# Eleven projections computed feature-major, and layer norms from chunk statistics

## The chip, the cores and the metric

The kernel runs on one core of a Trainium2 chip, in one launch. The metric is the device time of that launch in microseconds. All engine times below come from one profiled execution.

## The reference

Two blocks run one after the other on the same tokens (T = 256, model width 2048), in fp32. The first norms its input, projects it, and feeds a gated delta rule (8 heads of 128, causal convolution of 4 taps over q, k and v) and a block attention; both meet in a gated mix, an output projection and a feed-forward layer of width 5632. The second block has a differential attention layer and a forgetting attention layer, each followed by a layer norm. Cut to what the change touches:

```python
def _causal_short_conv(u, w):          # u: (1, T, 3072) = q, k, v projections of the delta rule
    y = up[:, 0:T] * w[0]              # up: u with three zero tokens in front
    for j in range(1, K):              # K = 4
        y = y + up[:, j:j + T] * w[j]
    return jax.nn.silu(y)
...
def layer_norm(x, g, b):
    mu = jnp.mean(xf, axis=-1, keepdims=True)
    var = jnp.mean(jnp.square(xf - mu), axis=-1, keepdims=True)
    y = (xf - mu) * lax.rsqrt(var + EPS)
    return (y * g + b).astype(x.dtype)
...
    sc = jnp.einsum('bqhcd,bkhcd->bhcqk', qb, k) + bias      # layer 0 of the second block (k2, q2)
    sc = jnp.einsum('bqhd,bkhd->bhqk', qb, k) + decay        # layer 1 (k3, q3)
...
    x = layer_norm(DN_ALPHA * x + gate[:, None] * y, ln_g[l], ln_b[l])
```

## The kernel before, in words

Every weight product runs in bodies of units. A unit is 256 rows by 512 columns of weights, 512 KB. SyncE loads it into one of four ring slots of `raw`; ScalarE rounds it to `w_hi` (`split`, L1105 to L1112), VectorE makes `w_lo = raw - w_hi` (L1704 to L1708), and TensorE multiplies both with the high and low parts of the operand, three fp32r matmuls per pair of tiles (`chunk`, L561 to L582). Ring slot j is free when TensorE has used unit j, so the splits run at most four units ahead. In its own slot j each engine first does the work hung there by a `between` function, then the split of unit j + 4.

`PLAN` (L340) lists the products: qkv (3 bodies of 16 units), spill (8), branch (4 of 8), w_out (2), ffn (11), down (2 of 44), then v2, k2, q2, g2, o2 for the first layer of the second block and v3, k3, q3, g3, o3 for the second, 2 bodies of 16 units each. A body makes 1024 output columns in two halves x = 0, 1 (accumulators `acc[0]`, `acc[1]`, two banks each, one for each 128 tokens). A plain product is token-major: the activations (128x128) are loaded as the stationary operand and 512 columns of weights stream.

The delta rule's q, k, v (qkv) and the attention's k and q (k2, q2, k3, q3) are needed feature-major. `turned_body` (L611) therefore copies each half to `stage` (`to_stage`, one bank on ScalarE, one on VectorE) and transposes it on TensorE in two groups of four 128x128 transposes (`turn_stage`, L550, `turn`, L529), in slot 11 for the first half and slot 3 of the next body for the second. From the turn banks ScalarE copies to `k_t`, `q_d` or `q_f` (`out_of_turn`, L1518); in qkv VectorE runs the convolution from them (`conv_pair`, L1815, slots 12, 13 and 4, 5) and ScalarE the silu (`silu_conv`, slots 14, 15 and 6, 7). `turn_free`, `turned` and `drained` count these steps.

The spill stage's mixer (`delta_net`, one `next` per slot on each engine) computes the delta rule beside the spill product; it starts with gates, root-mean-square norms of q and k (eight steps, each with an ACT square, a PE sum, an ACT root, a DVE reciprocal) and then the head groups.

`gemv` (L1710) adds one 128x512 tile per unit to a vector-matrix product; `mod_reduce` (L584) sums it with two matmuls.

`layer_tail` closes a layer: `residual_drain` (L2288) mixes the product into `xs`; ScalarE sums rows chunk by chunk (`row_sums`, L1571), VectorE makes the mean, ScalarE squares with accumulation (L1597) and takes the root, VectorE normalizes (L2343; the last layer L2334 and L2348, which feed the output DMAs). Ahead of v3, TensorE transposes normalized x (`turn_x`, L887), VectorE (`v3_operand`, L2232) and ScalarE (L1488) alternate in making the shifted and scaled blocks, then comes a thin product of 48 matmuls (`thin`, L642; 128x128 loaded, 256 columns) for the forget gate, then v3. `S2_SLOTS` are the slots of v3 in which the operand of q3 is transposed.

## Time and profile before

| | us |
|---|---|
| median of 3 runs | 2742.69 (2741.56 to 2744.43) |
| the profiled execution | 2742.39 |
| its span, first to last instruction | 2740.6 |
| TensorE matmul busy | 2631.8 (96%) |
| VectorE busy | 1839.4 (67%) |
| ScalarE busy | 1219.6 (45%) |
| chain that ended last, TensorE's share | 70% |

Busy time of an engine is the union of its instructions. A matmul's own duration (about 0.4 us) is longer than the spacing of two, since they are pipelined; the spacing of their starts tells the cost. A row of the timeline gives start and duration, and in brackets how long the engine idled before it and which instruction released it. PE is TensorE, PEld its weight loads, DVE VectorE, ACT ScalarE, SP SyncE.

### The profile page before, as it was taken

The numbers are of one execution on the slowest core, as the hardware profiler recorded it, in microseconds if no ns is written. First come the engines' busy times: TensorE is split into PE (matmuls) and PEld (weight loads), VectorE is DVE, ScalarE is ACT, GpSimd is POOL, SyncE is SP. The second block draws the span as 40 slices with busy tenths as digits, with TensorE's granted clock in tenths as the row PEclk, the third lists the DMA queues.
The fourth block names the chain that finished last, engine by engine and source line by source line (L and its number), as shares of the span: only waits on it lengthen the run. The fifth ranks groups of instructions, "written<-read, shape, count | busy, mean of one in ns | idle before, by whom it ended". The sixth has DMA issues, their size and how long they took to land.

```text
span 2740.6 us, 34109 instructions
## 1 busy us (share of the span) xinstructions
PE 2631.8 (96%) x12005; PEld 2120.9 (77%) x12005; DVE 1839.4 (67%) x2362; ACT 1219.6 (45%) x1575; POOL 0.2 (0%) x4
## 2 busy tenths in 40 slices
PE   7998999999699999999999999999999979999997
PEld 5775887887578788787878788788887768888875
DVE  5889866766567767777777666775477555545655
ACT  4445333334434444444443334444476444444553
POOL 0000000000000000000000000000000000000000
PEclk9999999999999999999999999999999989999998
DMA  6776767777357788888888777887645635665463
GB/s 221 234 243 206 232 212 225 229 231 271 127 181 238 253 271 273 271 274 268 274 270 267 243 252 247 276 271 235 180 143 183 189 126 168 198 209 167 125 220 124
DMA packets 312711, 604.66 MB, mean 221 GB/s; under 512 B 26590, under 2 KB 28644, under 8 KB 310668
## 3 DMA queue, kind: packets, MB, share of 16 engines
q1 hardware_dynamic: 301628, 571.92, 66.3%
q10 hardware_dynamic: 10960, 31.10, 3.0%
q8 instruction: 77, 1.26, 0.2%
q14 instruction: 46, 0.38, 0.0%
HBM read 592.31 MB, written 10.62 MB: 220 GB/s over the span
## 4 chain that ended last, share of the span: by engine, by line
PE 70%; DVE 2%; ACT 1%; DMA 0%; issue 0%; DVEq 0%; ACTq 0%
PE bank L577 22%; PE bank L579 22%; PE bank L578 22%; PE bank L539 2%; PE bank L958 1%; DMA gates<-spill 0%; PE bank L969 0%; PE bank L979 0%; PE bank L955 0%; PE bank L981 0%; PE bank L980 0%; ACT w_hi L1112 0%; DVE w_lo L1708 0%; PE bank L835 0%; PE bank L836 0%
## 5 line engine op out<-in xcount | busy, mean ns | idle before, releaser
L1708 DVE TENSOR_TENSOR w_lo<-raw,w_hi 128x1024 fp32r<-128x1024 f32 x820 | 1002.4, 1224 | 803.2 <-ACT w_hi L1112 788.6
L1112 ACT CAST w_hi<-raw 128x1024 fp32r<-128x1024 f32 x820 | 860.1, 1050 | 1377.0 <-PE bank L579 1312.9
L577 PE MATMUL bank<-w_hi,u_hi 128*128 128x512 f32 x1408 | 572.2, 406 | 10.3 <-DVE w_lo L1708 8.1
L579 PE MATMUL bank<-w_hi,u_lo 128*128 128x512 f32 x1408 | 561.2, 399 | 0.0
L578 PE MATMUL bank<-w_lo,u_hi 128*128 128x512 f32 x1408 | 561.2, 399 | 0.0
L577 PE MATMUL bank<-w_hi,s_hi 128*128 128x512 f32 x1280 | 514.6, 402 | 0.0
L579 PE MATMUL bank<-w_hi,s_lo 128*128 128x512 f32 x1280 | 507.3, 396 | 0.0
L578 PE MATMUL bank<-w_lo,s_hi 128*128 128x512 f32 x1280 | 507.0, 396 | 0.0
L1733 DVE SCALAR_TENSOR_TENSOR gemv_acc<-gemv_w,small,gemv_acc 128x512 f32<-128x512 f32 x480 | 358.1, 746 | 16.1 <-DMA gemv_w<-in_w_mod 15.2
L577 PEld LDWEIGHTS bank<-w_hi,u_hi 128*128 128x128 f32 x1408 | 267.6, 190 | 82.2 <-DVE w_lo L1708 13.3
L579 PEld LDWEIGHTS bank<-w_hi,u_lo 128*128 128x128 f32 x1408 | 267.3, 190 | 65.3
L578 PEld LDWEIGHTS bank<-w_lo,u_hi 128*128 128x128 f32 x1408 | 267.8, 190 | 62.4 <-issue 1.2
L579 PEld LDWEIGHTS bank<-w_hi,s_lo 128*128 128x128 f32 x1280 | 241.1, 188 | 58.6
L577 PEld LDWEIGHTS bank<-w_hi,s_hi 128*128 128x128 f32 x1280 | 241.1, 188 | 56.4 <-issue 0.5
L578 PEld LDWEIGHTS bank<-w_lo,s_hi 128*128 128x128 f32 x1280 | 241.4, 189 | 55.7
L577 PE MATMUL bank<-w_hi,hid_hi 128*128 128x512 f32 x352 | 140.0, 398 | 0.0
L579 PE MATMUL bank<-w_hi,hid_lo 128*128 128x512 f32 x352 | 139.5, 396 | 0.0
L578 PE MATMUL bank<-w_lo,hid_hi 128*128 128x512 f32 x352 | 139.5, 396 | 0.0
L577 PEld LDWEIGHTS bank<-w_hi,hid_hi 128*128 128x128 f32 x352 | 66.3, 188 | 16.4 <-issue 0.6
L579 PEld LDWEIGHTS bank<-w_hi,hid_lo 128*128 128x128 f32 x352 | 66.3, 188 | 16.2
L578 PEld LDWEIGHTS bank<-w_lo,hid_hi 128*128 128x128 f32 x352 | 66.3, 188 | 15.9
L577 PE MATMUL bank<-w_hi,mix_hi 128*128 128x512 f32 x128 | 51.1, 399 | 0.0
(336 smaller groups left out, 2060.1 us busy)
## 6 DMA issues: line engine op xcount, KB each, us to landing
gemv_w<-in_w_mod SPq DMA_DIRECT2D x384, 256.0 KB, 3.2
raw<-in_w_in SPq DMA_DIRECT2D x176, 512.0 KB, 4.4
raw<-in_a_w_in SPq DMA_DIRECT2D x128, 512.0 KB, 4.1
raw<-in_w_ffn_gate SPq DMA_DIRECT2D x88, 512.0 KB, 4.6
raw<-in_w_ffn_up SPq DMA_DIRECT2D x88, 512.0 KB, 4.4
raw<-in_w_ffn_down SPq DMA_DIRECT2D x88, 512.0 KB, 4.4
gemv_w<-in_kv_w_mod SPq DMA_DIRECT2D x128, 256.0 KB, 3.5
raw<-in_kv_w SPq DMA_DIRECT2D x64, 512.0 KB, 3.7
```

Source lines behind the costliest of these rows:

```text
L539: ins = pe.transpose(b[:, f * T + th * P:f * T + (th + 1) * P], src(f, th), ident)
L577: pe.matmul(o, xh, w_hi[:, s, t], start=(k == 0), stop=False)
L578: pe.matmul(o, xh, w_lo[:, s, t], start=False, stop=False)
L579: ins = pe.matmul(o, xl, w_hi[:, s, t], start=False, stop=(k == 2 * units - 1))
L958: ins = pe.matmul(b[:, P:3 * P], queries_of[p][:, a, P:T], k_t[:, a, 0:T], start=True, stop=not mask)
L1112: act.copy(w_hi[:, s], raw[:, s]).then_inc(hi_done, 1)
L1708: dve.tensor_tensor(w_lo[:, s], raw[:, s], w_hi[:, s].bitcast(F32), ALU.subtract).then_inc(lo_done, 1)
L1733: dve.scalar_tensor_tensor(out=gemv_acc[:], in0=w_k, scalar=c_k, in1=gemv_acc[:], op0=ALU.mult, op1=ALU.add).then_inc(gemv_step, 1)
```

## The change

Products qkv, k2, q2, k3 and q3 run through `across_chunk`: a 128x128 block of weights is the stationary operand and the 256 tokens stream, so the accumulators hold features by tokens. For each pair of tiles there are 12 matmuls of 256 columns instead of 6 of 512. The staging copies, the transposes and `out_of_turn` of these products are gone; ScalarE and VectorE drain one bank each straight to `k_t`, `q_d` or `q_f`, and the convolution reads the accumulators, in slots 9, 11 and 1, 3; the silu runs in slots 12, 14 and 4, 6. In the layer norms VectorE takes statistics of each 512-column chunk with `bn_stats` and joins them with `bn_aggr`; row sums and square passes on ScalarE are gone. Ahead of v3 only chunks 0 and 1 are normalized and transposed; chunks 2 and 3 follow in v3's units 0 and 1, the blocks in units 0 to 3, and the thin product after unit 8. `S2_SLOTS` move. The diff, cut to its core (call sites, removed arguments and most removed lines of `turned_body`, `turned_product` and the old `v3_operand` left out):

```diff
@@ -338,10 +339,10 @@
-            ("qkv", 3, 16, 4), ("spill", 8, 16, 0), ("branch", D // COLS, 8, 2), ("w_out", 2, 16, 0),
+            ("qkv", 3, 16, 0), ("spill", 8, 16, 0), ("branch", D // COLS, 8, 2), ("w_out", 2, 16, 0),
...
-            ("v2", 2, 16, 0), ("k2", 2, 16, 4), ("q2", 2, 16, 4), ("g2", 2, 16, 0), ("o2", 2, 16, 0),
-            ("v3", 2, 16, 0), ("k3", 2, 16, 4), ("q3", 2, 16, 4), ("g3", 2, 16, 0), ("o3", 2, 16, 0),
+            ("v2", 2, 16, 0), ("k2", 2, 16, 0), ("q2", 2, 16, 0), ("g2", 2, 16, 0), ("o2", 2, 16, 0),
+            ("v3", 2, 16, 0), ("k3", 2, 16, 0), ("q3", 2, 16, 0), ("g3", 2, 16, 0), ("o3", 2, 16, 0),
@@ -386,7 +387,7 @@
-        S2_SLOTS = (3, 9, 15, 21)
+        S2_SLOTS = (6, 11, 16, 21)
@@ -581,6 +582,26 @@
+            def across_chunk(pr, i, x, hi, lo, between):
+                if not (isinstance(i, int) and pr.body0 + i == 0):
+                    pe.wait_ge(drained[x], i * 2 + 2 * pr.body0)
+                half = pr.units // 2
+                for u in range(half):
+                    j = x * half + u
+                    pe.wait_ge(lo_done, i * pr.units + (pr.unit0 + j + 1))
+                    s = j % RING
+                    for t in range(2):
+                        k = 2 * u + t
+                        for f in range(4):
+                            o = acc[x][f // 2][:, f % 2 * T:(f % 2 + 1) * T]
+                            wh, wl = w_hi[:, s, t, f * P:(f + 1) * P], w_lo[:, s, t, f * P:(f + 1) * P]
+                            pe.matmul(o, wh, hi[:, k], start=(k == 0 and f % 2 == 0), stop=False)
+                            pe.matmul(o, wh, lo[:, k], start=False, stop=False)
+                            ins = pe.matmul(o, wl, hi[:, k], start=False, stop=(k == 2 * half - 1 and f % 2 == 1))
+                    ins.then_inc(w_used, 1)
+                    between(j)
@@ -608,23 +629,17 @@
+            def across_body(name, i, hi, lo, between=None):
...
+                    mod_due(pr, i, j)
...
+                for x in range(2):
+                    across_chunk(pr, i, x, hi, lo, due)
@@ -804,9 +819,7 @@
             for i in range(pr.bodies):
-                def due(j, i=i):
-                    if i == 0 and j == 3:
-                        turn_stage(products["qkv"], products["qkv"].bodies - 1, 1)
+                def due(j):
@@ -1032,9 +1042,9 @@
             for i in range(2):
-                turned_body("k2", i, s_hi, s_lo)
+                across_body("k2", i, s_hi, s_lo)
             for i in range(2):
-                turned_body("q2", i, s_hi, s_lo, products["k2"] if i == 0 else None)
+                across_body("q2", i, s_hi, s_lo)
@@ -1054,21 +1064,28 @@
-            for c in range(4):
-                pe.wait_ge(signal("ln_out"), 4 + c + 1)
-                turn_x(products["v3"], c, lambda q, c=c: (signal("h_odd"), c) if q else (signal("h_block"), 8 + c))
-            pe.wait_ge(turn_free, products["v3"].turn0)
-            pe.wait_ge(signal("ws_split"), 2)
-            thin(ws2_hi, ws2_lo, s_hi, s_lo).then_inc(signal("logits"), 1)
+            pr = products["v3"]
+            def turn_normed(c):
+                pe.wait_ge(signal("ln_out"), HALVES * (c + 1))
+                turn_x(products["v3"], c, lambda q: (signal("h_odd"), c) if q else (signal("h_block"), 8 + c))
+            turn_normed(0)
+            turn_normed(1)
...
+                    if i == 0 and j < 2:
+                        turn_normed(2 + j)
+                    if i == 0 and j == 8:
+                        pe.wait_ge(signal("ws_split"), 2)
+                        thin(ws2_hi, ws2_lo, s_hi, s_lo).then_inc(signal("logits"), 1)
...
-                plain_body("v3", i, s_hi, s_lo, due)
+                plain_body("v3", i, s_hi, s_lo, due, {q: pr.ahead0 + q + 1 for q in range(8)} if i == 0 else None)
@@ -1190,13 +1204,13 @@
-                act.wait_ge(turn_free, i * 4 + (pr.turn0 + q + 1))
+                act.wait_ge(drained[q // 2], i * 2 + (2 * pr.body0 + q % 2 + 1))
...
-                for q, at_ in ((2, 6), (3, 7)):
+                for q, at_ in ((2, 4), (3, 6)):
@@ -1204,11 +1218,11 @@
                         silu_before(j, i - 1)
-                    for q, at_ in ((0, 14), (1, 15)):
+                    for q, at_ in ((0, 12), (1, 14)):
...
-                body("qkv", i, to_stage, between)
+                body("qkv", i, nothing, between)
@@ -1488,20 +1502,26 @@
+                if q % 2 and q > 1:
+                    odd_block(q)
...
+            def odd_block(q):
+                pr, blocks = products["v3"], h_stage(q)
+                act.wait_ge(turned, pr.ahead0 + q + 1)
+                if q >= 4:
+                    act.wait_ge(turn_free, pr.ahead0 + q - 3)
+                for f in range(2):
+                    k = 2 * q + f
+                    ins = act.activation(blocks[:, f], bank[TURN + q % 2][:, f * T:(f + 1) * T], ACT.Identity,
+                                         scale=modc[:, 96 + KD + k:96 + KD + k + 1], bias=modc[:, 96 + k:96 + k + 1])
+                ins.then_inc(signal("h_odd"), 1)
@@ -1515,30 +1535,14 @@
+            def across_product(name, dst, scale):
+                def across_drain(pr, i, x):
+                    act.activation(dst[:, 8 * i + 4 * x:8 * i + 4 * x + 2], acc[x][0][:].rearrange("p (f t) -> p f t", f=2),
+                                   ACT.Copy, scale=scale).then_inc(drained[x], 1)
+                for i in range(products[name].bodies):
+                    body(name, i, across_drain)
@@ -1568,19 +1572,8 @@
-                def row_sums(c):
-                    act.wait_ge(signal("x_mixed"), 8 * layer + 2 * c + 2)
-                    for th in range(HALVES):
-                        part = slice(c * COLS, (c + 1) * COLS)
-                        act.activation(ln_tmp[layer][:, th, part], xs[:, th, part], ACT.Copy,
-                                       accum_out=sm(RCP + 8 + 4 * th + c)).then_inc(signal("row_sums"), 1)
...
                     def between(j, i=i):
-                        for c, at_ in ((2 * i - 1, 3), (2 * i, 11)):
-                            if j == at_ and c >= 0:
-                                row_sums(c)
@@ -1590,13 +1583,8 @@
                 own.link(act.activation(ln_tmp[layer][:, 0, D - 1:D], sm(E5, 1), ACT.Sqrt, bias=sm(E5, 1)))
-                row_sums(3)
-                act.wait_ge(signal("row_sums"), 8 * (layer + 1))
-                act.wait_ge(signal("mean"), layer + 1)
-                for th in range(HALVES):
-                    own.link(act.activation(ln_tmp[layer][:, th], xs[:, th], ACT.Square, bias=sm(RCP + 2 + th),
-                                            accum_out=sm(SS + th)))
-                    root(0, sm(SS + th), sm(RR + th), 1.0 / D, E5, "root_ln")
+                act.wait_ge(signal("moments"), layer + 1)
+                root(0, small[:, LN_MOMENTS + 1:LN_MOMENTS + 2 * HALVES:2], sm(RR, HALVES), 1.0, E5, "root_ln")
@@ -1666,11 +1652,15 @@
             layer_tail("o2", "d", 0, forget_weights)
-            for q in range(8):
+            odd_block(1)
+            for q in range(2):
...
                 def between(j, i=i):
-                    if i == 0 and j == 8:
+                    if i == 0 and j < 3:
+                        v3_operand(2 * j + 2)
+                        v3_operand(2 * j + 3)
+                    if i == 0 and j == 10:
@@ -1813,9 +1800,9 @@
             def conv_pair(pr, i, q):
-                n = pr.turn0 + q
-                dve.wait_ge(turned, i * pr.turns + (n + 1))
-                b = bank[TURN + q % 2]
+                x = q // 2
+                dve.wait_ge(w_used, i * pr.units + (pr.unit0 + (x + 1) * pr.units // 2))
+                b = acc[x][q % 2]
@@ -1830,11 +1817,11 @@
-                ins.then_inc(turn_free, 1)
+                ins.then_inc(drained[x], 1)
...
-                for q, at_ in ((2, 4), (3, 5)):
+                for q, at_ in ((2, 1), (3, 3)):
@@ -1842,11 +1829,14 @@
                         conv_before(j, i - 1)
-                    for q, at_ in ((0, 12), (1, 13)):
+                    for q, at_ in ((0, 9), (1, 11)):
...
-                body("qkv", i, to_stage, between)
+                body("qkv", i, nothing, between)
+            def nothing(pr, i, x):
+                pass
@@ -2229,22 +2216,21 @@
+            def even_block(q):
...
+                dve.wait_ge(turned, pr.ahead0 + q + 1)
+                for f in range(2):
+                    k = 2 * q + f
+                    ins = dve.tensor_scalar(h_stage(q)[:, f], bank[TURN][:, f * T:(f + 1) * T],
+                                            modc[:, 96 + KD + k:96 + KD + k + 1], modc[:, 96 + k:96 + k + 1], ALU.mult, ALU.add)
+                ins.then_inc(signal("h_block"), 1)
+            def block_low(q):
+                dve.wait_ge(turn_hi, products["v3"].cut_ahead0 + q + 1)
+                dve.tensor_tensor(s_lo[:, 2 * q:2 * q + 2], h_stage(q), s_hi[:, 2 * q:2 * q + 2].bitcast(F32),
+                                  ALU.subtract).then_inc(turn_free, 1)
@@ -2282,6 +2268,14 @@
+            def across(dst, scale):
+                def across_drain(pr, i, x):
+                    dve.tensor_scalar(dst[:, ds(i * 8 + 4 * x + 2, 2)], acc[x][1][:].rearrange("p (f t) -> p f t", f=2),
+                                      scale, None, ALU.mult).then_inc(drained[x], 1)
+                return across_drain
@@ -2295,6 +2289,10 @@
                                              op1=ALU.add).then_inc(signal("x_mixed"), 1)
+                layer, chunk = int(pr is products["o3"]), 2 * i + x
+                for th in range(HALVES):
+                    dve.wait_ge(signal("x_mixed"), 8 * layer + 2 * chunk + th + 1)
+                    own.inc(dve.bn_stats(sm(LN_STATS + 24 * th + 6 * chunk, 6), xs[:, th, chunk * COLS:(chunk + 1) * COLS]))
@@ -2323,31 +2321,34 @@
-                dve.wait_ge(signal("row_sums"), 8 * (layer + 1))
-                own.link(dve.tensor_reduce(sm(RCP + 2, HALVES), sm(RCP + 8, 8).rearrange("p (t c) -> p t c", t=HALVES), AX.X, ALU.add))
-                dve.tensor_scalar(sm(RCP + 2, HALVES), sm(RCP + 2, HALVES), -1.0 / D, None, ALU.mult).then_inc(signal("mean"), 1)
-                dve.wait_ge(signal("mean"), layer + 1)
+                own.wait()
+                for th in range(HALVES):
+                    ins = dve.bn_aggr(sm(LN_MOMENTS + 2 * th, 2), sm(LN_STATS + 24 * th, 24))
+                ins.then_inc(signal("moments"), 1)
+                dve.wait_ge(signal("moments"), layer + 1)
...
+                    own.inc(dve.scalar_tensor_tensor(out=x_last[:, 0], in0=xs[:, 0], scalar=sm(LN_MOMENTS),
+                                                     in1=lng_bc[1][:], op0=ALU.subtract, op1=ALU.mult))
+                dve.wait_ge(signal("root_ln"), layer + 1)
+                own.link(dve.reciprocal(sm(RR, HALVES), sm(RR, HALVES)))
+                if layer:
...
-                        own.inc(dve.scalar_tensor_tensor(out=x_last[:, th], in0=xs[:, th], scalar=sm(RCP + 2 + th),
-                                                         in1=lng_bc[1][:], op0=ALU.add, op1=ALU.mult))
+                        for half in range(2):
+                            part = slice(half * D // 2, (half + 1) * D // 2)
+                            dve.scalar_tensor_tensor(out=x_last[:, th, part], in0=x_last[:, th, part], scalar=sm(RR + th),
+                                                     in1=lnb_bc[1][:, part], op0=ALU.mult, op1=ALU.add).then_inc(
+                                signal("x_out"), 1)
+                        if th == 0:
+                            own.link(dve.scalar_tensor_tensor(out=x_last[:, 1], in0=xs[:, 1], scalar=sm(LN_MOMENTS + 2),
+                                                              in1=lng_bc[1][:], op0=ALU.subtract, op1=ALU.mult))
+            def normalized(c):
+                part = slice(c * COLS, (c + 1) * COLS)
...
-                    dve.wait_ge(signal("root_ln"), HALVES * layer + th + 1)
-                    own.link(dve.reciprocal(sm(RR + th), sm(RR + th)))
-                    if layer == 0:
-                        for c in range(4):
-                            part = slice(c * COLS, (c + 1) * COLS)
-                            dve.tensor_scalar(xs[:, th, part], xs[:, th, part], sm(RCP + 2 + th), sm(RR + th), ALU.add,
-                                              ALU.mult).then_inc(signal("ln_out"), 1)
-                        continue
-                    for half in range(2):
-                        part = slice(half * D // 2, (half + 1) * D // 2)
-                        dve.scalar_tensor_tensor(out=x_last[:, th, part], in0=x_last[:, th, part], scalar=sm(RR + th),
-                                                 in1=lnb_bc[1][:, part], op0=ALU.mult, op1=ALU.add).then_inc(
-                            signal("x_out"), 1)
+                    dve.tensor_scalar(xs[:, th, part], xs[:, th, part], sm(LN_MOMENTS + 2 * th), sm(RR + th), ALU.subtract,
+                                      ALU.mult).then_inc(signal("ln_out"), 1)
@@ -2466,8 +2467,8 @@
             body("v2", 1, value_drain)
-            plain("k2", to_stage)
-            plain("q2", to_stage)
+            plain("k2", across(k_t, 1.0))
+            plain("q2", across(q_d, SCALE))
@@ -2484,9 +2485,28 @@
             layer_tail("o2", "d", 0, o2_due)
-            v3_operand()
+            normalized(0)
+            normalized(1)
+            even_block(0)
+            block_low(0)
...
                 def between(j, i=i):
+                    if i == 0 and j == 0:
+                        even_block(2)
+                        block_low(1)
+                        normalized(2)
+                        block_low(2)
+                    if i == 0 and j == 1:
+                        normalized(3)
+                        even_block(4)
+                        block_low(3)
+                    if i == 0 and j == 2:
+                        block_low(4)
+                        even_block(6)
+                        block_low(5)
+                    if i == 0 and j == 3:
+                        block_low(6)
+                        block_low(7)
```

## Rows read from the trace of the kernel before

**Rows 1.** Two lines of the page: busy time (section 1) and a weight load (section 5).
```profile
PE 2631.8 (96%) x12005; PEld 2120.9 (77%) x12005; DVE 1839.4 (67%) x2362; ACT 1219.6 (45%) x1575; POOL 0.2 (0%) x4
...
L577 PEld LDWEIGHTS bank<-w_hi,u_hi 128*128 128x128 f32 x1408 | 267.6, 190 | 82.2 <-DVE w_lo L1708 13.3
```

**Rows 2.** Windows: us, busy us per engine (xcount), clock, DMA share, GB/s.
```profile
36.64:181.53 144.89, 142.52 (x622) 113.85 (x621) 118.64 (x172) 57.37 (x63) 0.00 (x0) 0.99 0.75 246
130.22:181.53 51.31, 49.24 (x211) 38.96 (x210) 44.97 (x69) 20.25 (x23) 0.00 (x0) 0.97 0.75 245
1079.07:1125.39 46.32, 46.32 (x204) 37.15 (x203) 33.73 (x39) 19.45 (x21) 0.00 (x0) 1.00 0.85 271
1794.70:1982.09 187.39, 187.39 (x832) 150.91 (x830) 108.83 (x112) 79.44 (x89) 0.00 (x0) 1.00 0.74 228
2223.49:2316.92 93.43, 93.43 (x418) 75.63 (x417) 51.76 (x58) 38.15 (x42) 0.00 (x0) 1.00 0.61 191
2316.92:2503.35 186.43, 186.43 (x827) 150.56 (x826) 93.96 (x82) 81.19 (x90) 0.00 (x0) 1.00 0.64 192
```

**Rows 3.** Timeline of TensorE in k2: start us, us, instruction.
```profile
1877.18 0.40 PE L578 MATMUL bank<-w_lo,s_hi 128*128 128x512 f32 x1
...
1899.20 0.40 PE L579 MATMUL bank<-w_hi,s_lo 128*128 128x512 f32 x1
```

**Rows 4.** Timeline of TensorE, the thin product ahead of v3, then v3.
```profile
2214.96 0.58 PE L646 MATMUL bank<-s_hi,ws_hi 128*128 128x256 f32 x1 [3.00 <-DVE s_lo L2246]
...
2221.69 0.28 PE L646 MATMUL bank<-s_hi,ws_hi 128*128 128x256 f32 x1
...
2223.49 0.39 PE L577 MATMUL bank<-w_hi,s_hi 128*128 128x512 f32 x1
```

**Rows 5.** Timeline of TensorE, its waits around qkv and spill; [idle before <-releaser].
```profile
135.09 0.50 PE L577 MATMUL bank<-w_hi,u_hi 128*128 128x512 f32 x1 [1.91 <-DVE w_lo L1708]
...
186.70 0.79 PE L577 MATMUL bank<-w_hi,u_hi 128*128 128x512 f32 x1 [2.20 <-DVE w_lo L1708]
...
188.14 0.63 PE L577 MATMUL bank<-w_hi,u_hi 128*128 128x512 f32 x1
188.57 0.63 PE L578 MATMUL bank<-w_lo,u_hi 128*128 128x512 f32 x1
...
277.20 0.47 PE L702 MATMUL bank<-keep,conv_out 128*128 128x128 f32 x1 [8.18 <-DVE k_dec L1981]
```

**Rows 6.** Timeline of VectorE in qkv and the first spill bodies.
```profile
129.88 0.87 DVE L1826 TENSOR_SCALAR conv_out<-bank,cols 128x256 f32 x2
...
133.82 1.22 DVE L1708 TENSOR_TENSOR w_lo<-raw,w_hi 128x1024 fp32r<-128x1024 f32 x1
...
135.62 1.22 DVE L1708 TENSOR_TENSOR w_lo<-raw,w_hi 128x1024 fp32r<-128x1024 f32 x1
...
193.01 0.48 DVE L1867 TENSOR_SCALAR gates<-bank,small 8x256 f32<-8x256 f32 x1
...
203.85 3.35 DVE L1889 RECIPROCAL sq<-sq 128x512 f32<-128x512 f32 x1
...
271.94 0.68 DVE L1971 TENSOR_TENSOR decay<-g_rows,small 128x512 f32<-128x512 f32 x1
```

**Rows 7.** Timelines of TensorE, VectorE and ScalarE between o2 and v3.
```profile
2202.87 1.94 PE L539 MATMUL bank<-keep,xs 128*128 128x128 f32 x8 [10.91 <-issue]
...
2194.53 2.35 DVE L1708 TENSOR_TENSOR w_lo<-raw,w_hi 128x1024 fp32r<-128x1024 f32 x2
...
2199.97 1.92 DVE L2343 TENSOR_SCALAR xs<-xs,small 128x512 f32<-128x512 f32 x4
...
2197.25 2.00 ACT L1597 ACTIVATE ln_tmp<-xs,small 128x2048 f32<-128x2048 f32 x1 [1.19 <-DVE small L2328]
```

**Rows 8.** Timeline of VectorE in the last layer norm.
```profile
2727.63 4.62 DVE L2334 SCALAR_TENSOR_TENSOR x_last<-xs,small,lng_bc 128x2048 f32<-128x2048 f32 x2
...
2734.94 2.48 DVE L2348 SCALAR_TENSOR_TENSOR x_last<-x_last,small,lnb_bc 128x1024 f32<-128x1024 f32 x2
```

91 lines of the change are left out of this document (17 added, 74 removed).

## The prediction

> **What bounds the kernel now.** TensorE is busy for 2631.8 of 2740.6 us [rows 1], so I read the profile from its side: first the busy table, then the stretches of the changed products, then the spacing of single matmuls, last the places where TensorE stands still. The profiled execution took 2742.39 us, 1.8 over its span and 0.30 under the median of 2742.69.
>
> In a weight product the matmuls start 234.3 ns apart: from 1877.18 to 1899.20 us there are 94 steps in 22.02 us [rows 3]. A body of 16 units has 192 of them, 45.0 us. The products k2 and q2 take 187.39 us for four bodies [rows 2]: 768 x 0.2343 = 179.9 us of matmuls, 3 gate-vector reductions of two matmuls (1.4), and 7 groups of 8 transposes. A group thus costs 0.86 us; those of k3 and q3 give (186.43 - 179.9 - 0.3) / 7 = 0.89 [rows 2]. I use 0.87. In these bodies nothing else is lost, so they are bound by TensorE alone.
>
> Three places are otherwise. The qkv stage takes 144.89 us [rows 2] against 134.9 of matmuls, 5 groups (4.4) and 2 reductions (0.9): 4.6 us are stalls, nearly all in the last two bodies, and they wait for VectorE's w_lo [rows 5]. The reason stands in VectorE's rows: a unit costs it 1.8 us of splitting and gate-vector work, a convolution pair 3.94 on top [rows 6], and two pairs in successive slots (12 and 13) take 11.5 us where TensorE needs 5.7. The next stage starts at 181.53 with VectorE behind: it reaches that stage's first mixer step at 193.01 only, then works without pause (two more convolution pairs, eight reciprocals of 3.35 us) until 271.94 [rows 6], and TensorE stands for 2.2 us at the start and 8.2 us at the end of it [rows 5]. Last, the layer norm between blocks: o2's last matmul ends at 2191.96 (the 10.91 us of idle before 2202.87), and v3 starts at 2223.49 [rows 4, 7].
>
> **The change, part by part.**
>
> *Pairs.* In 11 bodies (qkv 3, k2, q2, k3, q3 2 each) every matmul of 512 columns becomes two of 256, each with its own 128x128 weight load: 11 x 16 x 12 = 2112 old ones, 4224 new. The thin product of the kernel before has this very form (128x128 loaded, 256 columns, fp32r). At full clock it starts one each 120.0 ns: 15 steps from 2221.69 to 2223.49 [rows 4]. Two cost 240.0, 5.7 more than one of 512. That is 2112 x 5.7 = +12.1 us. Ends: half of 234.3 each would be +0; the upper end is a load that isn't hidden at all, 190 ns [rows 1], which is a rival below. I take 120.0, a row of the same form, though no stretch holds more than 29 of them in a row. VectorE and DMA were quiet in it, but the 512-column spacing is the same beside full DMA work and without.
> The thin matmuls at least show what a shorter matmul pays extra. The Trainium skill (TensorE: Matmul & The Clock Gate, Back-to-back issue gap) has N / 2.4 + 2.5 ns, which would make the pair 218.3 against 215.8 and this term +5.3; both its numbers are below the rows' 240.0 and 234.3, and the rows decide.
>
> *Transposes.* All 22 groups of these products go, with the copies to the staging tile on ScalarE and VectorE. 16 lie in k2, q2, g2's start, k3, q3 and g3's start, 5 in qkv: 21 x 0.87 = -18.3 us. The 22nd lies in the stretch that VectorE sets and is worth nothing by itself. The copies were hidden behind the next half's matmuls and stay so as drains of the same size: the accumulator is wanted again 8 units, 23 us, later.
>
> *Convolution.* It now reads the accumulators, in slots 9, 11 and 1, 3. Per body VectorE has 16 x 1.8 + 4 x 3.94 + 1.2 = 45.8 us of work against TensorE's 46.6 (384 x 0.120 + 0.5). A pair leaves it 2.9 us behind, the slot between gives 1.1 back, so it is at most 5.3 behind; four buffered units less the 2.2 us of splitting give some 6.4. I keep 1 us of stalls of 4.6: -3.6 (ends -4.6 and 0). The waits: VectorE's on the half's last unit has passed by slot 9 (the split of slot 8 waits for more); behind ScalarE's wait in slots 12, 14, 4, 6 stands its split, and the convolution is two or three slots old by then. TensorE's wait on the drained accumulator is new in kind: the last pair ends some 19 us into the next body, wanted at 23; behind it stands everything, so this margin of 4 us is the cover.
> The weights' DMA isn't the bound: a body of the feed-forward stage moves as much in 46.32 us without a stall at 271 GB/s [rows 2].
>
> *Start of the spill stage.* With the pairs out of slots 12 and 13, VectorE is about 4 us behind TensorE at the stage's start instead of 193.01 - 181.53 = 11.5. The work until the group start stays: 32.4 of units, 8 of convolutions, 31.8 for eight reciprocals with their products, 4.8 of small ones, 77 us against 78.9 measured. So this stretch ends at 81 to 83 us instead of 90.4 after the stage's start: -8 (ends -3, if the idle gaps of ScalarE's table loads grow since one silu moves beside an exp, and -9).
>
> *Layer norm between the blocks.* Before: residual, two last splits until 2196.9 [rows 7], mean, then ScalarE's square passes of 2.0 us each, normalized chunks from 2199.97, first transposes at 2202.87 [rows 7], thin product from 2214.96 for 8.53 us, mostly at the lower clock [rows 4]. After: the statistics are two bn_stats per chunk. No row has that instruction; between a one-pass tensor_scalar of 0.48 [rows 7] and two passes I take 0.61, and 0.2 for an aggregate. So splits end at 2198.1, aggregates 2198.5, root and reciprocal 2199.1, first chunk 2200.1. Transposes, even block (1.0), odd block (1.0), cast (0.6), low part (0.7) in order give the first operand at 2204.6, and v3 starts there, 18.9 us earlier. Back go: the thin product inside v3 at full clock 5.8, two transposed chunks 1.8, twelve matmuls at 1.2 GHz (0.43 us apart after a stall [rows 5], instead of 0.234) 2.3, and one wait of 1.4 for odd block 5, which ScalarE makes only after VectorE's block 4. Later units find their operands: block 7's low part is due at about 2226 and read at 2230. v3's 93.43 us [rows 2] become about 104.7, ending at 2309.3 instead of 2316.92: -7.6 (ends -2, if each of the first eight units waits, and -10, without the cold unit). Behind VectorE's waits for the transposes stand its splits, behind ScalarE's for the blocks its own; the buffered four units, 11 us, cover them.
>
> *Last layer norm.* 4.6 us of full-width products and ScalarE's squares ran side by side [rows 8]. Now: bn_stats 1.2, aggregates 0.4, product 2.3, two halves 2.5, product 2.3, two halves 2.5 from 2725.8: the last ends at 2737.1 instead of 2737.4. -0.3 (ends -0.8 and +1). The first three chunks' bn_stats fall in VectorE's 1.6 us pauses.
>
> Sum: +12.1 - 18.3 - 3.6 - 8 - 7.6 - 0.3 = -25.7; 2742.4 - 25.7 = 2716.7, or 2717.0 beside the median.
>
> **Rivals.**
> *A, short pairs are supplied more slowly than the array takes them.* The 29 short ones came after slow ones at half clock, during which a queue could fill. If over long stretches one comes each 124 ns, the pairs cost 2112 x (248 - 234.3) = +28.9 and the time is 2734. Against it: no spacing above 120.0 in those rows. The Trainium skill (same page, Step-by-step: what each phase is for) gives about 62 ns of sequencer work per MATMUL with hardware decoding off; taken for the load too, that is the 124.
> *B, the gains off the pure matmul path don't arrive.* VectorE has only 2% to spare per qkv body, and in v3 TensorE waits in order for blocks that two engines pass to each other. If parts 3 to 5 give nothing: 2742.7 + 12.1 - 18.3 - 0.3 = 2736. For it: VectorE's 44.97 busy us in the last qkv body [rows 2]. Against: the moved pairs give room exactly where it was behind.
> *C, slower: the weight load is not hidden in a long stream.* The decisive spacing is 126.1 ns, where the pairs cost 37.8 us and eat all. The load's own 190 ns as spacing would make 2112 x (380 - 234.3) = +308 and about 3012. Against it: the same loads lie hidden in the thin product, lasting as long.
> *D, nothing at all*: gains and pair cost cancel, 2737 to 2748, for instance A and B together.
>
> **Chances.** Forecast 0.66, A 0.12, B 0.12, C 0.06, D 0.04. The forecast's own range is 2708 to 2727 from the ends above; with A and B the range is 2705 to 2737. The bound for a measurable difference is 0.2%, 5.5 us: 2737.2. Faster 0.85 (forecast, A, most of B), same 0.08, slower 0.07.
>
> **What would show it.** Starts of the short matmuls 120.0 ns apart in k2; four bodies of k2 and q2 in about 185.7 us; qkv in 140 us without waits for w_lo in bodies 1 and 2; the first mixer step some 4 us after the spill stage's start and the group start 81 to 83 after it; v3's first matmul 13 us after o2's last, v3 lasting 105; the last 17 us unchanged. I am wrong if that spacing is 124 or more, if convolutions still make TensorE wait, or if v3's first eight units each show a wait.

## The result, and the profile after

The changed kernel takes 2723.69 us (median of 6 runs, 2721.84 to 2724.62) against 2742.07 (6 runs) for the kernel before: ratio 0.9932, 95% interval 0.9919 to 0.9945, 18.4 us faster. The forecast was 2717.0, 25.7 us below. The profiled execution took 2724.53 us against 2742.39, so 17.9 us are to be found, and 7.8 us of the forecast are missing.

Of the page of the changed kernel, the span and the busy times; [rows 1] holds the same of before:

```profile
span 2722.7 us, 37883 instructions
PE 2619.7 (96%) x13941; PEld 2208.6 (81%) x13941; DVE 1844.2 (68%) x2370; ACT 1183.8 (43%) x1496; POOL 0.2 (0%) x4
```

The "eleven projections" of the title are eleven bodies of five products (qkv 3, k2, q2, k3 and q3 2 each). TensorE's busy time fell by 12.1 us only; the other 6 us of gain are idle time that went away. Where it went is seen by stages: busy time of each engine in the stretches qkv, spill bodies 0 and 1, k2 with q2, v3, and k3 with q3 (columns: stretch, length, busy of each engine with its instructions, granted clock, DMA share, GB/s):

```profile
core 0: us, PE busy (x) PEld busy (x) DVE busy (x) ACT busy (x) POOL busy (x), PEclk, DMA share, GB/s
36.75:182.42 145.67, 140.64 (x1158) 139.02 (x1157) 119.44 (x175) 55.91 (x59) 0.00 (x0) 1.00 0.73 241
182.42:312.80 130.38, 113.90 (x481) 87.17 (x479) 121.14 (x139) 72.00 (x86) 0.00 (x0) 0.92 0.68 228
1788.87:1974.54 185.67, 185.67 (x1544) 184.99 (x1542) 108.91 (x112) 72.46 (x75) 0.00 (x0) 1.00 0.74 230
2197.26:2301.96 104.70, 103.16 (x480) 84.36 (x481) 60.25 (x75) 44.35 (x54) 0.00 (x0) 0.98 0.56 171
2301.96:2486.68 184.72, 184.72 (x1539) 184.56 (x1538) 94.06 (x82) 74.44 (x76) 0.00 (x0) 1.00 0.63 194
```

Against [rows 2]: k2 and q2 went from 187.39 to 185.67 us, k3 and q3 from 186.43 to 184.72, v3 from 93.43 to 104.70 with its start 26.2 us earlier. Spill bodies 0 and 1 took 68.67 + 68.27 = 136.94 us and now 130.38. But qkv went from 144.89 to 145.67, where 140 had been forecast. It alone makes 5.4 us of the 7.8 that are missing.

The short matmuls, a stretch of k2 (start, duration, line, tiles, shape). Their starts lie 120 ns apart to the end of the body:

```profile
1840.09 0.28 PE L599 MATMUL bank<-s_hi,w_hi 128*128 128x256 f32 x1
1840.21 0.29 PE L600 MATMUL bank<-s_lo,w_hi 128*128 128x256 f32 x1
1840.33 0.28 PE L601 MATMUL bank<-s_hi,w_lo 128*128 128x256 f32 x1
1840.45 0.28 PE L599 MATMUL bank<-s_hi,w_hi 128*128 128x256 f32 x1
```

In qkv TensorE waits for VectorE again. The waits of TensorE in the stage, then those of VectorE in body 1, then in body 2 (waiting line, releaser, us in total, times, longest):

```profile
PE bank L599 <- DVE w_lo L1698: 5.0, 5, 1.5
...
DVE gemv_acc L1723 <- DMA gemv_w<-in_w_mod: 3.9, 3, 1.6
DVE gemv_hi L1721 <- DMA gemv_w<-in_w_mod: 1.5, 1, 1.5
DVE conv_out L1815 <- DVE conv_out L1815: 1.4, 8, 0.2
DVE conv_out L1815 <- DVE conv_out L1813: 0.8, 4, 0.2
...
DVE gemv_acc L1723 <- DMA gemv_w<-in_w_mod: 2.0, 3, 1.2
...
DVE gemv_hi L1721 <- DMA gemv_w<-in_w_mod: 0.6, 1, 0.6
```

And the two bodies by themselves:

```profile
82.83:133.10 50.27, 47.47 (x388) 46.50 (x387) 42.58 (x65) 19.51 (x21) 0.00 (x0) 1.00 0.75 244
133.10:182.42 49.32, 47.09 (x388) 46.44 (x387) 44.10 (x67) 19.59 (x21) 0.00 (x0) 1.00 0.76 256
```

Add up body 1 from these rows: VectorE is busy for 42.58 us, waits 5.4 for gate-vector tiles that are still on their way, and 2.2 between the steps of its convolution chains. That is 50.2 of 50.27 us: VectorE has no slack at all in this body, although it is busy for only 85% of it. A body of TensorE's work is 46.5 us. Without the 5.4 us of waits for a DMA VectorE's sum would lie under it, at 44.8. Where they fall is seen in its timeline, ahead of the first pair of the body (start, duration, in brackets the idle time before and its releaser):

```profile
85.39 0.75 DVE L1723 SCALAR_TENSOR_TENSOR gemv_acc<-gemv_w,small,gemv_acc 128x512 f32<-128x512 f32 x1 [1.57 <-DMA gemv_w<-in_w_mod]
...
88.76 0.75 DVE L1721 SCALAR_TENSOR_TENSOR gemv_hi<-gemv_w,small,gemv_acc 128x512 fp32r<-128x512 f32 x1 [1.49 <-DMA gemv_w<-in_w_mod]
```

These are steps of successive slots, 3.4 us apart, where VectorE needs 1.8 us for a unit and TensorE uses one in 2.9. VectorE is behind after the pairs of body 0 and should catch up here; held by the tiles, it falls further behind.

### The profile page after: what moved, and what is told of

Same layout as the page of the kernel before. It is cut to its first block, busy times and chain, and to the rows that moved or that the text cites. A ratio compares the mean times of both kernels' runs of the same rounds, so it can differ in the third digit from the quotient of the medians.

```text
span 2722.7 us, 37883 instructions
## 1 busy us (share of the span) xinstructions
PE 2619.7 (96%) x13941; PEld 2208.6 (81%) x13941; DVE 1844.2 (68%) x2370; ACT 1183.8 (43%) x1496; POOL 0.2 (0%) x4
## 4 chain that ended last, share of the span: by engine, by line
PE 70%; DVE 2%; ACT 1%; issue 1%; DMA 0%; DVEq 0%; ACTq 0%
PE bank L578 17%; PE bank L579 17%; PE bank L580 17%; PE bank L599 5%; PE bank L601 5%; PE bank L600 4%; PE bank L540 2%; PE bank L971 1%; DMA gates<-spill 0%; ACT w_hi L1129 0%; PE bank L982 0%; DVE w_lo L1698 0%; PE bank L992 0%; PE bank L968 0%; PE bank L994 0%
## 5 line engine op out<-in xcount | busy, mean ns | idle before, releaser
L578 PE MATMUL bank<-w_hi,s_hi 128*128 128x512 f32 x768 | 311.4, 405 | 1.2 <-DVE w_lo L1698 1.1
L580 PE MATMUL bank<-w_hi,s_lo 128*128 128x512 f32 x768 | 304.9, 397 | 0.0
L579 PE MATMUL bank<-w_lo,s_hi 128*128 128x512 f32 x768 | 304.8, 397 | 0.0
L599 PE MATMUL bank<-s_hi,w_hi 128*128 128x256 f32 x1024 | 289.5, 283 | 0.0
L600 PE MATMUL bank<-s_lo,w_hi 128*128 128x256 f32 x1024 | 288.3, 282 | 0.0
L601 PE MATMUL bank<-s_hi,w_lo 128*128 128x256 f32 x1024 | 288.3, 282 | 0.0
L600 PEld LDWEIGHTS bank<-s_lo,w_hi 128*128 128x128 f32 x1024 | 193.3, 189 | 0.2
L601 PEld LDWEIGHTS bank<-s_hi,w_lo 128*128 128x128 f32 x1024 | 193.2, 189 | 0.0
L599 PEld LDWEIGHTS bank<-s_hi,w_hi 128*128 128x128 f32 x1024 | 191.9, 187 | 0.6 <-issue 0.3
L579 PEld LDWEIGHTS bank<-w_lo,s_hi 128*128 128x128 f32 x768 | 145.3, 189 | 32.7
```

Of the source, the lines that this page charges most:

```text
L578: pe.matmul(o, xh, w_hi[:, s, t], start=(k == 0), stop=False)
L579: pe.matmul(o, xh, w_lo[:, s, t], start=False, stop=False)
L580: ins = pe.matmul(o, xl, w_hi[:, s, t], start=False, stop=(k == 2 * units - 1))
L599: pe.matmul(o, wh, hi[:, k], start=(k == 0 and f % 2 == 0), stop=False)
L600: pe.matmul(o, wh, lo[:, k], start=False, stop=False)
L601: ins = pe.matmul(o, wl, hi[:, k], start=False, stop=(k == 2 * half - 1 and f % 2 == 1))
```

## The experiments

The theory after reading the trace: the convolution pairs were moved to better slots, but VectorE enters them without the lead that the forecast gave it, because on the way it waits for gate-vector tiles. The rivals: the pairs lie too densely; or the DMA's rate sets how fast VectorE catches up.

**Four gate-vector buffers in qkv.** Two more buffers in the staging tile, which the stage no longer uses:

```diff
+            if pr is products["qkv"]:
+                s = k % 4
+                return (gemv_w[:, s] if s < 2 else stage[:, 1, s - 2]), wide_landed[s]
```

> Against the changed kernel, whose qkv bodies take 46.08, 50.27 and 49.32 us: the gate-vector tiles of the qkv stage go through four buffers instead of two (the other two lie in the staging tile, which is free there). Theory 1, recovery is limited by the gate-vector ring: after a convolution pair VectorE could do a unit in 1.8 us, but it waits for gemv_w (9 waits, 8.2 us in bodies 1 and 2), and SyncE, which waits for the ring, holds the next weight load back by up to 3.7 us. Then VectorE's waits for gemv_w in the stage go to under 2 us, bodies 1 and 2 fall to at most 48 us each, the first mixer step comes 4 to 6 us after the spill stage's start instead of 8.2, and the time is 3 to 6 us below the changed kernel's (ratio to before 0.991 to 0.992). Theory 2, the convolution pairs lie too densely: the waits for gemv_w go, but TensorE's waits for w_lo after each second pair stay and the bodies stay within 0.7 us. Theory 3, the DMA's rate sets the recovery: the waits move from gemv_w to raw, nothing gets shorter.

Measured: 2718.23 us, ratio 0.9907 (0.9891 to 0.9924), 5.5 us below the changed kernel. Bodies 1 and 2:

```profile
82.91:131.36 48.45, 47.03 (x389) 46.39 (x388) 42.10 (x65) 19.54 (x21) 0.00 (x0) 1.00 0.75 249
131.36:178.20 46.84, 46.84 (x389) 46.40 (x388) 43.71 (x67) 19.61 (x21) 0.00 (x0) 1.00 0.80 269
```

4.3 us are gone from the two bodies, and body 1 stays a little above the 48 us expected. VectorE's waits for these tiles fell from 8.2 us to 4.8, not to under 2, and the first mixer step still comes 8.5 us after the spill stage's start. With four buffers a tile also took longer to land: 4.5 to 4.7 us (median) after its issue, where it took 3.1 in the changed kernel. The ring of two is part of the cause; 1.9 us of body 1 are left with four buffers.

**Pairs four slots apart.**

```diff
-                for q, at_ in ((2, 1), (3, 3)):
+                for q, at_ in ((2, 1), (3, 5)):
-                    for q, at_ in ((0, 9), (1, 11)):
+                    for q, at_ in ((0, 9), (1, 13)):
```

> The changed kernel with the convolution pairs four slots apart (9 and 13, 1 and 5) instead of two, silu one slot later for the second of each. Theory 2 (pairs too dense): the slot group between gives VectorE 3 units of 1.1 us back instead of one, so TensorE's waits for w_lo of 1.1 to 1.5 us after the second pair go; bodies 1 and 2 fall from 50.27 and 49.32 to about 47.5, the time by 3 to 5 us. Theory 1 (gate-vector ring): recovery at 2.5 instead of 1.8 us a unit is only 0.4 us a unit against TensorE's 2.9, so 1 to 2 us at most are gained. Theory 3 (DMA rate): as theory 1.

Measured: 2720.47 us, 0.9918 (0.9901 to 0.9934). The two bodies by windows:

```profile
83.17:131.54 48.37, 46.94 (x388) 46.30 (x387) 43.25 (x67) 18.90 (x21) 0.00 (x0) 1.00 0.77 260
131.54:180.22 48.68, 47.03 (x386) 46.40 (x386) 43.89 (x67) 19.40 (x21) 0.00 (x0) 1.00 0.75 259
```

What TensorE waits for in the stage:

```profile
PE bank L599 <- DVE conv_out L1815: 2.0, 3, 0.9
```

2.5 us are gone from the two bodies and 3.2 from the time; the bodies were expected at about 47.5. (The same qkv code differs by up to 1.9 us between executions, as the last run shows, so the 2.5 alone are thin; the medians carry the reading.) TensorE no longer waits for w_lo at all, but the later pair now releases the accumulator too late: with VectorE behind, the cover of 4 us that the forecast gave the drained accumulator is used up. So the density counted too, and it is not the whole either.

**Both.**

> Four gate-vector buffers in qkv and pairs four slots apart together. Theory 1: as with four buffers alone, within 1.5 us. Theory 2: as with the pairs apart alone. If the two add up, both hold: bodies 1 and 2 at about 46.6 us, the qkv stage at 139.5 us instead of 145.67 and the time 6 to 8 us below the changed kernel's.

Measured: 2716.7 us, 0.9904 (0.9887 to 0.992), 7.0 us below the changed kernel. The stage takes 139.14 us, and TensorE waits for nothing in it. The two bodies by windows:

```profile
82.84:129.36 46.52, 46.52 (x388) 46.29 (x387) 43.26 (x66) 19.51 (x21) 0.00 (x0) 1.00 0.83 272
129.36:175.90 46.54, 46.54 (x388) 46.31 (x387) 43.61 (x67) 19.64 (x21) 0.00 (x0) 1.00 0.82 271
```

VectorE's waits in the first of them, all of them:

```profile
DVE conv_out L1829 <- DVE conv_out L1829: 1.4, 8, 0.2
DVE w_lo L1708 <- ACT w_hi L1139: 1.0, 2, 0.7
DVE conv_out L1829 <- DVE conv_out L1827: 0.8, 4, 0.2
```

The two edits gave 4.3 and 2.5 us of body time alone and 6.5 together. VectorE does the same work, but no wait for a gate-vector tile is left, and 43.26 + 2.2 us fit under 46.5. The DMA moves 272 GB/s in the first of these bodies instead of 244: its rate was not the limit, so the third theory falls.

**Half of the convolution.** Taps 3 and 2 only.

```diff
-                for tap in range(TAPS - 1, -1, -1):
+                for tap in range(TAPS - 1, 1, -1):
```

> The changed kernel with two of the convolution's four taps left out (so q, k and v of the delta rule are others): a pair costs VectorE about 1.9 us instead of 3.94. If VectorE's convolution work is what TensorE waits for in the bodies 1 and 2 of qkv, their 50.27 and 49.32 us fall to 46.6 to 47.2 whatever limits the recovery; the first mixer step of the spill stage comes 3 to 5 us after its start instead of 8.2. If weights or gate-vector tiles arrive late by themselves, they stay above 48.

Measured, one run: 2709.8 us. Bodies 1 and 2 take 46.53 and 46.54 us with the ring of two and the dense slots left as they were, and the first mixer step comes 4.7 us after the spill stage's start. VectorE waits for no gate-vector tile either. These are all its waits in the stage:

```profile
DVE w_lo L1698 <- ACT w_hi L1129: 33.9, 30, 7.3
DVE conv_out L1815 <- DVE conv_out L1813: 2.0, 8, 0.6
```

Waiting for ScalarE's w_hi is the wait of an engine that keeps up. So the tiles are late only where VectorE, behind by its convolution work, comes through its slots faster than the ring is filled again. The ring of two makes no stall with half the load. The full load made one with four buffers too, 1.9 us in body 1, as long as the pairs lay two slots apart; it takes the wider slots as well to be rid of it.

**Weights or gate-vector tile?** While SyncE waits for a gate-vector buffer, it also holds back the next load of weights. Two issues of weights in the changed kernel lay 4.0 us apart (86.89 and 90.93), and the wait of SyncE for the ring lay between them. To part the two, GpSimd issues the gate-vector loads:

```diff
+        @block.gpsimd
+        def _(pool):
+            for i in range(pr.bodies):
+                for k in range(KD):
+                    if i or k >= 2:
+                        pool.wait_ge(gemv_step, i * KD + k - 1)
+                    pool.dma_start(gemv_w[:, k % 2], w_mod_2[0][k * P:(k + 1) * P, ...]).then_inc(wide_landed[k % 2], 16)
```

> The changed kernel with the 48 gate-vector loads of qkv issued by GpSimd instead of SyncE, still into two buffers. It parts the two ways in which the ring of two costs time. If it is the weights that suffer (SyncE waits for the ring and issues the next weight load up to 3.7 us late, which the 4.2 us of four buffers gave back), bodies 1 and 2 fall from 50.27 and 49.32 us towards the 48.45 and 46.84 of four buffers although VectorE's waits for gemv_w stay at 6 to 8 us. If it is VectorE's own wait for the gate-vector tile (3.5 us from issue to landing, two buffers), they stay within 0.7 us, or grow if GpSimd's loads take longer to land.

Measured: 2730.43 us, 0.9956 (0.9939 to 0.9972), 6.7 us above the changed kernel. Bodies 1 and 2 by windows:

```profile
83.06:134.54 51.48, 47.52 (x388) 46.51 (x387) 43.52 (x66) 19.49 (x21) 8.34 (x16) 1.00 0.73 235
134.54:187.78 53.24, 47.56 (x389) 46.50 (x388) 44.11 (x67) 19.37 (x21) 8.62 (x17) 1.00 0.73 238
```

The gate-vector loads of the stage (tile, queue, count, size, median us from issue to landing):

```profile
gemv_w<-in_w_mod POOLq DMA_DIRECT2D x45, 256.0 KB, 4.1
```

ScalarE's waits for weights fell from 53.4 us to 29.2 in these bodies, and the bodies still grew by 5.1 us; VectorE's waits for the tile rose from 8.2 us to 13.4, with a landing after 4.1 us instead of 3.1 (the 3.5 of the expectation was too high). So the time follows VectorE's own wait for the tile and not ScalarE's for the weights. What GpSimd's issue would bring at an equal landing time stays open.

**Only k2, q2, k3 and q3 feature-major**, on the kernel before, with `across_chunk` and `across_product` as in the change:

```diff
-                turned_body("k2", i, s_hi, s_lo)
+                across_body("k2", i, s_hi, s_lo)
-            plain("k2", to_stage)
+            plain("k2", across(k_t, 1.0))
```

> The kernel before with only k2, q2, k3 and q3 feature-major; qkv and the layer norms stay as they were. Theory (each short pair costs 5.7 us per thousand more than one 512-column matmul, each transposed group 0.87 us): 1536 x 0.0057 = +8.8 and 16 x 0.87 = -13.9, together -5.2 us, ratio 0.9981; k2 and q2 in 185.7 us instead of 187.39, k3 and q3 in 184.7 instead of 186.43, g2 and g3 0.9 shorter each, qkv unchanged at 144.9. Rival (the short matmuls run at 120.0 ns only because other parts of the changed kernel leave TensorE's neighbours idle, supplied at 124 ns otherwise): 1536 x 0.0137 = +21, so +7 us, ratio 1.0026.

Measured: 2735.5 us, 0.9975 (0.9964 to 0.9985). k2 and q2:

```profile
1794.48:1980.15 185.67, 185.67 (x1543) 184.98 (x1542) 109.48 (x112) 72.46 (x75) 0.00 (x0) 1.00 0.74 230
```

k3 and q3 take 184.72 us, g2 56.65 instead of 57.53 and g3 62.45 instead of 63.34. The sum of the stages is -1.7 - 0.9 - 1.7 - 0.9 = -5.2 us, the forecast's number. The qkv stage, with the code of before, took 145.40 us instead of 144.89. A further 1.0 us came from the thin product: in this execution 17 of the spacings of its 48 matmuls were at half clock, some 213 ns, before they fell to 120 at full clock, where [rows 4] comes from an execution with 28. The rival with 124 ns is out.

**Everything ahead of v3 again**, with the statistics kept. TensorE's side is below; VectorE makes all blocks ahead of v3 too, but in the changed kernel's order, with the chunks 2 and 3 normalized between blocks, where the kernel before normalized all four chunks first:

```diff
-            turn_normed(0)
-            turn_normed(1)
+            for c in range(4):
+                turn_normed(c)
+            pe.wait_ge(turn_free, pr.turn0)
+            pe.wait_ge(signal("ws_split"), 2)
+            thin(ws2_hi, ws2_lo, s_hi, s_lo).then_inc(signal("logits"), 1)
```

> The changed kernel with all four chunks normalized and transposed and the thin product computed ahead of v3, as before; the chunk statistics stay. Theory (the statistics bring 2 to 3 us, the late chunks and the thin product inside v3 the rest): first transposes still some 8.2 us after o2's last matmul, v3's first matmul 28 to 29 us after it instead of 12.5 (before: 31.5), v3 93.4 us instead of 104.7, so k3 starts 4.5 to 5.5 us later than in the changed kernel. Rival (the statistics carry the whole gain, what moves into v3 is only paid elsewhere): k3 starts within 1 us of the changed kernel's.

Measured: 2730.77 us, 0.9954 (0.9938 to 0.997), 7.1 us above the changed kernel. The profiled execution lies 8.3 above the changed kernel's, and 1.9 of these are in qkv's body 2, which has the same code in both. Three of TensorE's rows between o2 and v3, from the timeline:

```profile
2194.74 1.94 PE L540 MATMUL bank<-keep,xs 128*128 128x128 f32 x8 [8.20 <-issue]
...
2201.45 1.97 PE L540 MATMUL bank<-keep,xs 128*128 128x128 f32 x8 [2.50 <-DVE xs L2345]
...
2209.10 0.58 PE L661 MATMUL bank<-s_hi,ws_hi 128*128 128x256 f32 x1 [2.54 <-DVE s_lo L2227]
```

And o2 with v3 as one stretch by windows, in this kernel:

```profile
2094.11:2310.21 216.10, 200.54 (x890) 162.31 (x889) 130.34 (x162) 86.65 (x100) 0.00 (x0) 0.94 0.55 176
```

in the kernel before:

```profile
2100.70:2316.92 216.22, 200.84 (x890) 162.77 (x889) 126.14 (x155) 96.17 (x121) 0.00 (x0) 0.95 0.56 176
```

and in the changed kernel:

```profile
2092.28:2301.96 209.68, 198.42 (x890) 160.39 (x889) 129.91 (x162) 86.37 (x100) 0.00 (x0) 0.97 0.57 181
```

The first transposes come 2.7 us earlier than before, as expected, but then TensorE waits 2.5 us for a chunk whose normalization VectorE does only between two blocks. v3 starts 30.2 us after o2's last matmul, not 28 to 29, where it started 31.5 after it before. Net of all, the statistics with this order of blocks gained 0.1 us: 216.10 against 216.22. Even that is not theirs: 19 matmuls of the thin product ran at half clock here and 28 before, which is worth 0.8 us, and a stall of 1.2 us in o2's first body, told of below, is in it. What the statistics would bring with all four chunks normalized first was not run. Starting v3 with two chunks and putting the thin product inside it brought 6.4 us, where 4.5 to 5.5 were expected. Half of my expectation fell with this, the 2 to 3 us for the statistics.

**A better version.** Both qkv edits, and two moves of VectorE's work:

```diff
-                if i == 0 and j == 8:
+                if i == 0 and j == 11:
                     mod_columns(1)
...
                         normalized(2)
                         block_low(2)
+                        normalized(3)
                     if i == 0 and j == 1:
-                        normalized(3)
                         even_block(4)
```

> Four gate-vector buffers and pairs four slots apart, and two moves of VectorE work: the gate columns in o2 from slot 8 to slot 11, away from the residual's drain and statistics in slot 7, and chunk 3's normalization in v3 from slot 1 to slot 0, ahead of that slot's split. Theory (VectorE's slot 7 and 8 of o2 hold 5.9 us of work in a row, and TensorE's transposes in v3 wait for the normalization behind a split that itself waits 3.1 us): o2's first body 47.3 to about 46.1 us, v3's first body 58.2 to 56.5, the rest as with both qkv edits, 2713 to 2715 us, ratio 0.989 to 0.990. If these waits only move to the next step of the same chains, it stays at 2716 to 2717.

Measured: 2713.34 us, 0.989 (0.9874 to 0.9906), 10.3 us below the changed kernel and 3.4 below the version with both edits. o2's first body and v3's first body:

```profile
2084.68:2130.65 45.97, 45.97 (x203) 37.06 (x202) 33.96 (x42) 20.28 (x22) 0.00 (x0) 1.00 0.68 229
2188.32:2244.36 56.04, 55.22 (x272) 45.82 (x273) 33.48 (x45) 24.50 (x32) 0.00 (x0) 0.99 0.52 169
```

o2's body lost 1.3 us against the version with both edits, as expected. v3's lost 2.1 where 1.7 were expected, but 1.2 of that is the clock: its first 3 matmuls here lay 0.43 us apart or more (half clock), the first 10 in the version with both edits. The edit itself brought 0.9 us: TensorE's wait of 0.7 us for one of VectorE's blocks is gone from the body. So the body came out near the forecast in part by luck, and of the 3.4 us between the two medians the trace shows 1.3 + 0.9 = 2.2 for the two moves.

**The changed kernel once more.**

> The changed kernel once more, unchanged, to see how much its qkv bodies differ from one execution to the next: the kernel with everything ahead of v3 had the same qkv code and took 50.26 and 51.25 us for bodies 1 and 2 where the changed kernel took 50.27 and 49.32. If the waits come from when transfers land, the sum of the two moves by 1 to 2 us again while all bodies of k2, q2, k3 and q3 repeat to 0.05 us.

Measured: 2724.53 us, 0.9939 (0.9922 to 0.9955). qkv bodies 1 and 2 took 50.54 and 50.70 us, together 101.2 after 99.6 and, in the kernel with everything ahead of v3, 101.5. The gain of four buffers in these bodies, 4.3 us against the first execution, is well beyond this spread; that of the wider slots alone, 2.5, is not far beyond it. The eight bodies of k2, q2, k3 and q3 repeated to 0.02 us. v3's first body took 56.25 us instead of 57.99. TensorE in the first 5.7 us of v3, by windows (length, busy, granted clock, DMA share, GB/s):

```profile
2199.47:2205.20 5.73, 5.73 (x29) 1.00 0.01 3
```

and in the first execution:

```profile
2197.26:2203.00 5.74, 5.74 (x21) 0.66 0.01 3
```

## Why the prediction was right, and where 7.8 us went

*Pairs and transposes: right, in mechanism and size.* 120.0 ns holds over whole bodies with VectorE, ScalarE and 230 GB/s of DMA beside it. The four products and the starts of g2 and g3 gave -5.2 us, forecast 1536 x 5.7 ns - 16 x 0.87 us = -5.2. Rival A and rival C are refuted. The Trainium skill (TensorE: Matmul & The Clock Gate, Back-to-back issue gap) gives N / 2.4 + 2.5 ns as the gap of isolated matmuls; the measured 120.0 and 234.3, in streams with a load for each matmul, lie above its 109.2 and 215.8, and the pair's price is 5.7 ns, not 2.5. The measurement decides. The Trainium skill's 62 ns of sequencer work for a matmul with hardware decoding off (same page, Step-by-step: what each phase is for), taken for the load as well, makes 124 by estimate; no run here shows the sequencer's part.

*Convolution in qkv: wrong, 5.4 us.* The forecast for the stage was 144.9 + 3.3 - 4.4 - 3.6 = 140.2, measured 145.67. The failed step is VectorE's budget of 45.8 us against 46.6 per body, and with it the recovery of 1.1 us for each unit between pairs. The durations in it were right (42.58 us busy in body 1 and 44.10 in body 2, with 2.2 and 2.1 between chained steps), but it held no wait for the gate-vector tile: two slots of body 1 without a pair took 3.4 us, not 1.8. The trace of before had that wait, 7.8 us over the same two bodies, in a row that I did not use, because I read VectorE's rows for what they cost and not for what stood in front of them:

```profile
DVE gemv_acc L1733 <- DMA gemv_w<-in_w_mod: 7.8, 8, 1.8
```

With it VectorE's sum for body 1 is 50.2 us against TensorE's 46.5, there is no lead of 6.4 us to spend on a pair, and 4 us of cover for the accumulator are thin. The pairs' place was the second half of it. Four buffers and wider slots each removed part, together all: 139.14 us, 1.1 better than the forecast.

Three readings beside it were off as well. "At most 5.3 behind" does not follow from its terms, which give 2 x 2.9 - 1.1 = 4.7. The lead of 6.4 is three units less the splitting, 3 x 2.9 - 2.2 = 6.5, not four. And of the 4.6 us called stalls of before only 2.4 are waits for w_lo (144.89 us with 142.52 busy); some 1.6 are seven matmuls 0.427 us apart, at half clock, and the steps beside them, right behind the longest wait of 1.9 us.

*Start of the spill stage: right in direction, 1.4 us short.* The first mixer step came 8.2 us after the stage's start, not 4: VectorE enters the stage behind, for the reasons above. Four buffers alone did not change that (8.5), wider slots alone brought 6.9. The last of the eight reciprocals, VectorE's row here, starts 78.5 us after the stage's start and did so 84.6 after it before:

```profile
260.96 3.35 DVE L1879 RECIPROCAL sq<-sq 128x512 f32<-128x512 f32 x1
```

That is -6.1, and bodies 0 and 1 lost 6.6, where 8 were forecast. VectorE's work for the head groups starts 84.3 us after the stage's start, not 81 to 83. With the two qkv edits the step comes at 5.4 and the reciprocal at 75.7; with half of the convolution at 4.7 and 71.8. Part of what is gained here is given back: with both edits spill body 2 starts 9.8 us earlier than in the changed kernel and branch body 1 only 7.3, since the last spill body grew from 105.39 to 107.76. What it waits for there was not tested.

*Layer norm between the blocks: -6.5 instead of -7.6.* The chain was as computed: first transposes after 8.20 us of idle, v3's first matmul 12.5 us after o2's last (forecast 12.6), v3 104.70 us (forecast 104.7). That v3 agrees to a tenth is luck in part: its first 9 matmuls ran at half clock, where 12 were forecast; in the second execution none did, v3 took 102.97 us, and the whole part gave -8.3. A pair of bn_stats took 1.28 us, 0.64 each (forecast 0.61), an aggregate 0.19. Missed was a stall of 1.2 us in o2's first body: the first chunk's statistics stand in VectorE's queue between the residual and the gate columns, and the split waits behind all of them. VectorE's row of the statistics, and TensorE's row after its wait:

```profile
2123.75 1.28 DVE L2295 BATCH_NORM_STATS2 small<-xs 128x6 f32<-128x512 f32 x2
...
2128.23 0.50 PE L578 MATMUL bank<-w_hi,s_hi 128*128 128x512 f32 x1 [1.07 <-DVE w_lo L1698]
```

Moving the columns three slots on removed it. I had named what waits behind VectorE in v3, but not in o2, where the instruction was added.

*Last layer norm: right.* From the end of o3's matmuls to the end 17.5 us before and 17.2 after.

*Rival B* (the gains off the pure matmul path don't arrive) held for qkv and not for the other two: VectorE's narrow margin was the reason I gave for it, and the reason was true. The sum of misses is 5.4 + 1.4 + 1.1 = 7.9 us against 7.8 in the profiled executions. The forecast's range of 2708 to 2727 is narrower than the ends it names: added up they reach from 2700 to 2733, and the measured 2723.7 lies in both.

## What to carry to other kernels

Budget an engine that must keep up with another by its busy time plus the waits in front of its instructions, by line and releaser: a wait for a DMA that costs nothing today fills the margin that the change means to use. Two matmuls of 256 columns in place of one of 512 cost 5.7 ns here and a group of eight transposes 0.87 us. A half of a body has 96 such pairs, 0.55 us, so a feature-major product paid in all of these; by the same two numbers, and as an estimate that no run here tested, it stops paying above some 150 pairs for each group saved. Add up everything that stands in one slot of the following engine, also the small work that was hung there for other reasons, before hanging something more in it.

## What was not expected of the hardware

- In k2 and q2 each matmul has a weight load of its own (the window holds 1542 loads and 1544 matmuls), and the loads are busy for 184.99 of 185.67 us. A load lasts some 190 ns, and still a matmul starts each 120.0 ns without a wait. Whether the 2.9 ns over half of 234.3 are the load's is not shown.
- After the same idle of 8.2 us and the same transposes, v3's matmuls started at half clock for 0 to 10 of them, from one execution to the next: a granted clock of 0.66 or 1.00 in its first 5.7 us, worth 1.7 us. Edits in that stretch can't be judged by one trace.
- The waits in qkv differ by up to 1.9 us between executions of the same code, while bodies bound by TensorE alone repeat to 0.02 us.
